# Routing inside the output projection: places taken tile by tile, first two experts' rows built on chip

## The chip, the cores and the metric

One core of a Trainium2 chip runs the kernel. The metric is the device time in microseconds (us), the median of several runs. TensorE (PE), VectorE (DVE), ScalarE (ACT), GpSimd (POOL) and SyncE (SP) run their own instruction streams and meet at semaphores. SP issues the weight DMAs.

## The reference, cut to what matters

Two layers, each a token mixer and a mixture of experts, over 512 tokens of width 1024:

```python
x = x + mix                                   # layer 0: convolution module, layer 1: attention
h = rms_norm(x, norm2_g[i])
x = x + hierarchical_moe(h, ...)              # best group of 4, then top 2 of its 8 experts
# per token and picked expert: gate * (silu(h @ w1[e]) * (h @ w3[e])) @ w2[e]
# 32 experts, each three matrices of 1024 x 512 (2 MB in float32), all float32
```

Both layers read all 96 expert matrices, about 200 MB each.

## The kernel before, in words

Tokens lie in NT = 4 tiles of 128. A weight unit is one 2 MB matrix. There are ten places for units: a ring of six, and four "extra" places that share memory with other data (`area3`, `hT`, `area1`, `area2`). SP issues unit loads in a fixed order; each waits until the work that used its place is done (`to_ring`, `to_extra` in `moe_weights`).

**The join of mixer and experts** (twice, once a layer). `mix_out` is the last projection of the mixer, in two halves of 512 columns, and per half four tiles of eight 512-wide matmuls (L1296). DVE adds each tile to the residual (`add_mix`, L931); ACT makes the norm (L627 to L633) and stores the normed rows `xn` to DRAM; PE transposes them (`transpose_xn`, L1197), DVE scales them into `hT` (`take_hT`, L846), and PE forms the routing logits of the tile (`logits`, L1313, L1314: 8 matmuls of 36 columns and one of the bias). After the logits of all four tiles `route` runs: DVE picks group and experts for all tiles at once (L945 to L976), PE counts ranks with triangular ones (L1322, L1325), DVE turns ranks into slots and lists (L979 to L1008), PE and DVE make the list of rows (L1329, L1011), and POOL gathers the rows of experts 0 and 1 from DRAM (L551). PE runs four matmuls to hold its clock (`stay_warm`, L1204), transposes the gathered rows (L1340), DVE copies them (L1034), and the first expert's matmuls start (`up`, L1350).

**The experts.** Each has 64 slots. A step of PE is `up` of expert e (32 matmuls, L1350), `hid_T` of e-1 (L1358), `rows_T` of e+1 (L1340), `down` of e-1 (L1367). ACT takes silu (L703) and the result (L707), POOL gathers rows (L529) and scatters results to DRAM (L540). Tokens over 64 in an expert go into extra tiles (`over_tile`); in these data layer 0 has one and layer 1 none. At the end ACT loads the results (L739) and DVE adds them (L1082).

Trace names: `banks` is PSUM, `scratch` and `area` are working memory, `ring` the ring of units.

## Time and profile before

| | us |
|---|---|
| median of 3 runs | 1643.52 (1643.09 to 1645.52) |
| the profiled execution | 1641.64 |
| its span, first to last instruction | 1639.5 |
| PE busy | 1389.2 (85% of the span) |
| DVE / ACT / POOL busy | 449.2 / 329.3 / 272.6 |

The two stretches in which all sixteen DMA engines are busy are the two expert stages. In between, and before the first, they stand almost idle. The mean granted PE clock is 0.932 of full.

### The profile page before, as it was taken

What the parts mean: (1) busy time and instruction counts of PE and PEld (TensorE: products, weight loads), DVE (VectorE), ACT (ScalarE), POOL (GpSimd) and SP (SyncE); (2) the same over time, 40 slices, a digit from 0 to 9 for tenths busy, and PEclk for the clock granted to TensorE, in tenths of its full rate; (3) what the DMA queues carried; (4) which work ended last, traced back from release to release, by engine and by line L of the source; (5) the groups of instructions that cost most, each with busy time, mean ns of one, the idle gap of its engine ahead of it and who ended that gap; (6) DMA issues with size and microseconds to landing.
All of it is one profiled execution on the core that took longest, in us unless ns stands there. A gap on an engine that the chain in (4) does not pass through costs nothing.

```text
span 1639.5 us, 16522 instructions
## 1 busy us (share of the span) xinstructions
PE 1389.2 (85%) x6006; PEld 631.7 (39%) x6006; DVE 449.2 (27%) x859; ACT 329.3 (20%) x638; POOL 272.6 (17%) x373
## 2 busy tenths in 40 slices
PE   6998896988888888884799999996998888888883
PEld 3443453333332232231556666544333233223231
DVE  1898424110110110110444544425111011011012
ACT  3564230110000000000444444421100000000000
POOL 3787001121111111110000000001121111111110
PEclk9999896998999999998899999996999999999997
DMA  8322046899999999999500401226899999999994
GB/s 293 93 103 103 0 154 247 362 425 426 426 427 426 426 426 424 424 375 356 204 0 1 154 1 52 103 90 264 351 409 427 426 427 426 426 417 424 415 425 193
DMA packets 62540, 473.63 MB, mean 289 GB/s; under 512 B 15800, under 2 KB 15800, under 8 KB 36512
## 3 DMA queue, kind: packets, MB, share of 16 engines
q1 hardware_dynamic: 49792, 443.63, 65.9%
q0 software_dynamic: 10400, 16.82, 2.7%
q10 hardware_dynamic: 2304, 12.58, 2.0%
q8 instruction: 29, 0.48, 0.1%
q14 instruction: 15, 0.12, 0.0%
HBM read 466.95 MB, written 23.33 MB: 299 GB/s over the span
## 4 chain that ended last, share of the span: by engine, by line
PE 50%; DMA 35%; DVE 7%; POOL 2%; issue 2%; ACT 2%; SPq 1%; ACTq 0%; POOLq 0%; DVEq 0%
DMA ring<-in_moe_w 33%; PE banks L1350 19%; PE banks L1460 6%; PE banks L1296 4%; PE banks L1367 4%; PE banks L1489 3%; POOL scratch L519 2%; DVE banks L892 2%; PE banks L1209 2%; PE banks L1282 2%; PE banks L1549 2%; PE banks L1504 1%; PE banks L1229 1%; DMA area<-y_dram 1%; PE banks L1313 1%
## 5 line engine op out<-in xcount | busy, mean ns | idle before, releaser
L1350 PE MATMUL banks<-ring,scratch 128*64 128x512 f32 x1984 | 493.7, 648 | 137.7 <-DMA ring<-in_moe_w 126.8
L1350 PEld LDWEIGHTS banks<-ring,scratch 128*64 128x64 f32 x1984 | 158.4, 148 | 469.4 <-issue 469.4
L1044 DVE COPY scratch<-banks 128x256 f32<-128x256 f32 x65 | 27.6, 425 | 786.9 <-PE banks L1358 786.9
L1367 PE MATMUL banks<-ring,scratch 128*64 128x512 f32 x1008 | 230.2, 598 | 3.0 <-DVE scratch L1044 3.0
L703 ACT ACTIVATE scratch<-banks 64x512 f32<-64x512 f32 x65 | 38.3, 589 | 585.5 <-PE banks L1350 585.5
L537 POOL COPY at_out<-rows_out 128x1 int32 (+1 forms) x64 | 11.7, 183 | 685.9 <-ACT scratch L707 685.9
L1460 PE MATMUL banks<-hT,ring 128*128 128x512 f32 x256 | 117.9, 604 | 0.8 <-DVE hT L846 0.8
L1209 PE MATMUL banks<-hT,ring 128*128 128x512 f32 x256 | 113.1, 601 | 5.3 <-DMA ring<-in_conv_w_in 5.3
L1367 PEld LDWEIGHTS banks<-ring,scratch 128*64 128x64 f32 x1008 | 68.1, 136 | 117.4 <-issue 110.4
L519 POOL TENSOR_TENSOR scratch<-scratch 128x512 f32<-128x512 f32 x77 | 98.0, 1274 | 23.2 <-ACT scratch L670 12.9
L707 ACT ACTIVATE scratch<-banks 128x512 f32<-128x512 f32 x65 | 38.8, 597 | 284.3 <-PE banks L1367 284.3
L892 DVE SCALAR_TENSOR_TENSOR banks<-scratch,chan,banks 128x512 f32<-128x512 f32 x119 | 79.1, 748 | 0.0
L540 POOL DMA_INDIRECT y_dram<-scratch,at_out x64 | 65.4, 1022 | 56.5 <-POOL at_out L537 56.5
L1209 PEld LDWEIGHTS banks<-hT,ring 128*128 128x128 f32 x256 | 48.8, 193 | 65.9 <-issue 65.8
L529 POOL DMA_INDIRECT scratch<-xn_dram,at_in x60 | 63.2, 1053 | 52.5 <-POOL at_in L526 47.7
L547 POOL MEMSET scratch<- 128x512 f32 x4 | 2.1, 525 | 418.5 <-DVE x_res L931 418.4
L670 ACT ACTIVATE scratch<-scratch,chan 128x512 f32<-128x512 f32 x84 | 58.3, 717 | 36.0 <-POOL scratch L519 25.4
L1460 PEld LDWEIGHTS banks<-hT,ring 128*128 128x128 f32 x256 | 46.2, 189 | 49.3 <-issue 46.9
L1489 PEld LDWEIGHTS banks<-ring,hT 128*128 128x128 f32 x512 | 59.0, 192 | 3.8 <-issue 3.8
L1296 PE MATMUL banks<-ring,area 128*128 128x512 f32 x136 | 59.6, 594 | 0.9 <-DVE area L1180 0.9
L1489 PE MATMUL banks<-ring,hT 128*128 128x128 f32 x512 | 59.6, 275 | 0.0
L1358 PEld LDWEIGHTS banks<-ident,scratch 64*128 64x128 f32 x260 | 35.9, 209 | 54.3 <-issue 54.3
(215 smaller groups left out, 1197.4 us busy)
## 6 DMA issues: line engine op xcount, KB each, us to landing
ring<-in_moe_w SPq DMA_DIRECT2D x187, 2048.0 KB, 20.8
area<-in_moe_w SPq DMA_DIRECT2D x6, 2048.0 KB, 12.2
ring<-in_attn_w_qkv SPq DMA_DIRECT2D x6, 2048.0 KB, 17.0
ring<-in_conv_w_in SPq DMA_DIRECT2D x4, 2048.0 KB, 14.2
area<-y_dram ACTq DMA_DIRECT2D x8, 1024.0 KB, 8.0
ring<-in_conv_w_out SPq DMA_DIRECT2D x2, 2048.0 KB, 21.2
xn_dram<-area ACTq DMA_DIRECT2D x8, 512.0 KB, 2.6
hT<-in_moe_w SPq DMA_DIRECT2D x2, 2048.0 KB, 7.7
```

Source lines behind the costliest of these rows:

```text
L519: g.tensor_tensor(pacc[ct % 2], pacc[ct % 2], tap[(k - 1) % TAP_BUFS], ALU.add).then_inc(tap_added, 1)
L529: g.indirect_dma_start(out=xe[s], out_offset=None, in_=xn_dram[l][:, :], in_offset=bass.IndirectOffsetOnAxis(ap=at_in[:, s:s + 1], axis=0) ...
L540: g.indirect_dma_start(out=y_dram[l][:, :], out_offset=bass.IndirectOffsetOnAxis(ap=at_out[:, s:s + 1], axis=0), in_=y_sb[s], in_offset=No ...
L670: a.activation(dst, u_buf[ct % 2][:, w:w + T], ACT.Copy, scale=chan[:, ct, w:w + 1]).then_inc(tap_made, 1)
L707: a.activation(y_sb[s], bank[6 + s][:], ACT.Copy).then_inc(sems["y_taken"], 1)
L892: ins = v.scalar_tensor_tensor(dst, ub[:, w:w + T], chan[:, ct, w:w + 1], acc, ALU.mult, ALU.add)
L1209: last = mm(dst, w[:, c, cols], src[:, c, :], start=start and c == 0, stop=stop and c == NC - 1)
L1296: last = mm(dst[:], src[:, c, t * P:(t + 1) * P], w_chunks(n0 + n)[:, c, :], start=c == 0, stop=c == NC - 1)
L1350: last = mm(bank[2 + s][q * SLOTS:(q + 1) * SLOTS, :], xeT[s][:, j, h, :], w[:, c, :], start=c == 0, stop=c == NC - 1)
L1367: last = mm(bank[6 + s][q * SLOTS:(q + 1) * SLOTS, :], hidT[s][:, j, :], w2c[:, j, q * 512:(q + 1) * 512], start=j == 0, stop=j == 3)
L1460: last = mm(qk_bank[c][:], w_chunks(u)[:, k, (h % 4) * P:(h % 4 + 1) * P], hT[:, k, :], start=k == 0, stop=k == NC - 1)
L1489: last = mm(v_bank[:, t * P:(t + 1) * P], hT[:, k, t * P:(t + 1) * P], w_chunks(u)[:, k, (h % 4) * P:(h % 4 + 1) * P], start=k == 0, stop= ...
```

## The change

What it does, in the order of the program:

- **Places.** The extra places are taken in another order. `hT` no longer serves the experts' routing, so it takes a unit as soon as the mixer has read it, and `area3` takes one when the mixer is done with it; `area2` at the end of the projection; `area1` after both the stores of `xn` and the building of the first rows.
- **Logits and picks tile by tile.** PE transposes the residual itself (not the normed rows), two matmuls into the next tile's projection, and makes the logits one matmul later. DVE scales the logits by the norm when it reads them and picks for one tile (`choose`, 16 instructions). The bias matmul is gone.
- **Ranks of tiles 0 and 1** are counted inside the last tile's projection, ahead of the logits of tile 2. DVE's `slots` makes their slots there.
- **First rows on chip.** The rows of experts 0 and 1 are no longer gathered from DRAM. `first_rows` builds them, already transposed, by matmuls of `xn` with a 0/1 matrix of 128 columns: 16 matmuls for tiles 0 and 1, 16 for tiles 2 and 3, after two 512-wide fp16 matmuls that clear two banks.
- **Warming matmuls:** four before; now one after the projection and one between the two parts of `first_rows`.
- **End of the experts.** `up` of the last expert is put ahead of `down` of the third last, and the last seven unit loads are reordered to fit. `last_scatter` copies its list column ahead of its wait for the result, not behind it.

PE at the end of the projection and in the routing, layer 0 (128x512 `ring,area` is the projection, `w_route` the logits), before:

```order
L1296 MATMUL banks_3<-ring,area 128x512 x8
L1197 MATMUL banks_7<-ident,area 128x128 x8
L1313 MATMUL banks_5<-w_route,hT 128x36 x8
L1314 MATMUL banks_5<-b_route,ones 128x36
L1197 MATMUL banks_7<-ident,area 128x128 x8
L1313 MATMUL banks_5<-w_route,hT 128x36 x8
L1314 MATMUL banks_5<-b_route,ones 128x36
L1313 MATMUL banks_5<-w_route,hT 128x36 x8
L1314 MATMUL banks_5<-b_route,ones 128x36
L1322 MATMUL banks_5<-scratch,before 128x32
```

and now, from the last tile's projection on:

```order
L1343 MATMUL banks_3<-ring,area 128x512
L1363 MATMUL banks_5<-w_route,scratch 128x36 x8
L1343 MATMUL banks_3<-ring,area 128x512 x5
L1251 MATMUL banks_3<-x_res,ident 128x512
L1245 MATMUL banks_7<-ident,x_res 128x128 x8
L1363 MATMUL banks_5<-w_route,scratch 128x36 x8
L1382 MATMUL banks_1<-ones,zero 128x512 x2
L1389 MATMUL banks_1<-scratch,area 128x128 x16
L1371 MATMUL banks_5<-scratch,ones 128x32 x2
L1371 MATMUL banks_5<-scratch,before 128x32
```

Three logits groups stood behind the projection but for one; now one does, and the row-building matmuls stand between it and the ranks.

PE from the lists to the first experts, before:

```order
L1329 MATMUL banks_5<-scratch 128x47 x8
L1333 MATMUL banks_7<-scratch 128x47 x8
L1204 MATMUL banks_7<-x_res,ident 128x512 x4
L1340 MATMUL banks_1<-ident,scratch 128x128 x8
L1350 MATMUL banks_3<-ring,scratch 64x512 x32
```

and now:

```order
L1375 MATMUL banks_5<-scratch,ones 128x32 x4
L1251 MATMUL banks_3<-x_res,ident 128x512
L1389 MATMUL banks_1<-scratch,area 128x128 x16
L1405 MATMUL banks_5<-scratch 128x47 x8
L1427 MATMUL banks_3<-ring,scratch 64x512 x16
```

Between the row list and the first `up` nothing is left; the transposes of gathered rows are gone and the second list stands behind the first `up`.

The diff, cut to what the prediction speaks of:

```diff
+                to_extra(2, w1_of(3), *((glu_ready, 8), (v_ready, HEADS))[l])
+                to_extra(0, w3_of(2), *((ln_done, NC), (oT_done, HEADS))[l])
                 to_ring(4, w2_of(0), *freed[4])
                 to_ring(5, w1_of(2), *freed[5])
-                to_extra(0, w3_of(2), mix_ready, 8 * (l + 1))
-                to_extra(1, w2_of(1), logits_ready, l + 1)
-                to_extra(2, w1_of(3), xn_stored, 16 * NT * (l + 1))
-                to_extra(3, w3_of(3), xe_loaded[l][1], 16)
+                to_extra(1, w2_of(1), mix_ready, 8 * (l + 1))
+                sp.wait_ge(xn_stored, 16 * NT * (l + 1))
+                to_extra(3, w3_of(3), main[l]["xT_ready"], 2)
...
+                def last_scatter(s, e, wait_at):
+                    pool.wait_ge(y_stored[l][s], 16 * (e // 2))
+                    g.tensor_copy(at_out[:, s:s + 1], rows_out[:, e:e + 1]).then_inc(at_copied[l], 1)
+                    pool.wait_ge(at_copied[l], wait_at)
+                    pool.wait_ge(m["y_taken"], e + 1)
...
                             ins.then_inc(x_done, 1)
+                            take_hT(N_MOE[l], t)
                             invert_rms(N_MOE[l], t)
-                            if t >= 1:
-                                take_hT(N_MOE[l], t - 1)
-                take_hT(N_MOE[l], NT - 1)
+                            if t == NT - 2:
+                                slots(l, 0, NT - 2)
+                            if t < NT - 1:
+                                choose(l, t)
...
+                            if n == 1 and t >= 1 and c == 1:
+                                transpose_xn(N_MOE[l], t - 1)
+                                if t == NT - 1:
+                                    ranks(l, 0, NT - 2)
+                            if n == 1 and t >= 1 and c == 2:
+                                logits(l, t - 1)
                         last.then_inc(mix_ready, 1)
-                        if n == 1 and t >= 1:
-                            transpose_xn(N_MOE[l], t - 1)
-                        if n == 1 and t >= 2:
-                            logits(l, t - 2)
+                stay_warm(1, warm_bank)
                 transpose_xn(N_MOE[l], NT - 1)
-                logits(l, NT - 2)
-                logits(l, NT - 1)
...
+            def first_rows(l, lo, hi):
+                if lo == 0:
+                    for b in range(2):
+                        mm(first_pair[l][:, b, :], zero16[:], ones16[:, 0:1].to_broadcast([P, 512]), ...)
+                pe.wait_ge(xn_done, 4 * N_MOE[l] + hi)
+                pe.wait_ge(hot_first_done, 2 * l + (1 if hi < NT else 2))
+                for j in range(4):
+                    for h in range(2):
+                        k = 2 * j + h
+                        for t in range(lo, hi):
+                            last = mm(first_pair[l][:, k // 4, ...], xn[:, t, ...], hot_first[:, t]..., ...)
             def route(l):
-                pe.wait_ge(picks_done, l + 1)
...
+                logits(l, NT - 1)
+                pe.wait_ge(x_done, 8 * l + NT)
+                pe.wait_ge(picks_done, NT * l + NT - 1)
+                first_rows(l, 0, NT - 2)
+                ranks(l, NT - 2, NT)
+                stay_warm(1, warm_bank)
+                first_rows(l, NT - 2, NT)
                 pe.wait_ge(hot_done, 2 * l + 1)
...
-                stay_warm(4, bank[7])
...
-                rows_step(0, 0)
-                rows_step(1, 1)
                 up_step(0, 0, in_ring(0), in_ring(1))
+                lists2(l)
...
-                step(EXPERTS - 2, 0, in_ring(MOE_UNITS - 7), in_ring(MOE_UNITS - 6), in_ring(MOE_UNITS - 5))
-
-                up_step(EXPERTS - 1, 1, in_ring(MOE_UNITS - 4), in_ring(MOE_UNITS - 3))
+                up_step(EXPERTS - 2, 0, in_ring(MOE_UNITS - 7), in_ring(MOE_UNITS - 6))
+                hid_T(m, 1, EXPERTS - 2)
+                rows_step(EXPERTS - 1, 1)
+                up_step(EXPERTS - 1, 1, in_ring(MOE_UNITS - 5), in_ring(MOE_UNITS - 4))
                 hid_T(m, 0, EXPERTS - 1)
+                down_step(EXPERTS - 3, 1, in_ring(MOE_UNITS - 3))
                 down_step(EXPERTS - 2, 0, in_ring(MOE_UNITS - 2))
```

On DVE the order of the routing is now, for all four tiles: `choose` of 0, 1, then `slots` of tiles 0 and 1, `choose` of 2 and 3, `slots` of 2 and 3, the lists as before, and a copy of each expert's first rows (`take_first`) behind `hot_done` and behind the row list.

## Rows read from the trace of the kernel before

**Rows 1.** Chain in order of time, layer 1 experts: start us, us, what.
```profile
1204.94 19.35 DMA ring<-in_moe_w
1224.52 8.80 PE banks L1350 x32
1233.92 21.70 DMA ring<-in_moe_w
```

**Rows 2.** Stretch sums: us, PE, PEld, DVE, ACT, POOL busy, PEclk, DMA share, GB/s.
```profile
1230.00:1605.00 375.00, 311.08 (x1358) 113.73 (x1356) 43.36 (x72) 28.46 (x48) 56.48 (x92) 0.94 1.00 420
```

**Rows 3.** Timeline, layer 1, projection's end to logits: start, us, engine, line, [idle before].
```profile
1108.12 0.69 DVE L931 TENSOR_TENSOR x_res<-x_res,banks 128x512 f32<-128x512 f32 x1 [6.48 <-PE banks L1296]
1108.87 1.87 PE L1313 MATMUL banks<-w_route,hT 128*128 128x36 f32 x16
...
1113.32 3.47 PE L1313 MATMUL banks<-w_route,hT 128*128 128x36 f32 x16
1113.57 0.69 DVE L846 TENSOR_TENSOR hT<-banks,norm_g 128x512 f32<-128x512 f32 x1 [0.16 <-PE banks L1197]
```

**Rows 4.** The same, layer 1, ranks to the first expert.
```profile
1128.33 0.29 DVE L979 COPY scratch<-banks 128x128 f32<-128x128 f32 x1 [0.58 <-PE banks L1325]
...
1128.88 0.39 DVE L982 TENSOR_TENSOR scratch<-scratch,steps 128x224 f32<-128x224 f32 x1
...
1129.99 0.19 DVE L985 TENSOR_TENSOR scratch<-scratch 128x32 f32<-128x32 f32 x1
1130.21 0.42 DVE L988 TENSOR_TENSOR scratch<-scratch 128x256 f32<-128x256 f32 x1
...
1135.59 0.55 DVE L1006 TENSOR_TENSOR scratch<-scratch,token 128x376 f16<-128x376 f16 x1
...
1143.37 13.95 PE L1350 MATMUL banks<-ring,scratch 128*64 128x512 f32 x64 [0.46 <-DVE scratch L1034]
```

**Rows 5.** Timeline, layer 0, the same two ends.
```profile
238.03 0.69 DVE L931 TENSOR_TENSOR x_res<-x_res,banks 128x512 f32<-128x512 f32 x1 [6.49 <-PE banks L1296]
...
274.92 0.65 PE L1350 MATMUL banks<-ring,scratch 128*64 128x512 f32 x2 [0.46 <-DVE scratch L1034]
```

**Rows 6.** Chain in order of time: 128-wide matmuls; a tile of the projection.
```profile
873.28 3.57 PE banks L1489 x32
...
1091.15 6.87 PE banks L1296 x16
```

**Rows 7.** Timeline, layer 1: transposes of one tile.
```profile
1107.92 1.12 PE L1197 MATMUL banks<-ident,area 128*128 128x128 f32 x8
```

**Rows 8.** Stretch sums, columns as in rows 2, round changes of the clock.
```profile
791.00:794.70 3.70, 3.29 (x14) 2.92 (x15) 2.34 (x6) 3.33 (x5) 0.00 (x0) 0.50 1.04 389
794.80:798.00 3.20, 2.42 (x8) 1.17 (x7) 2.51 (x10) 0.21 (x1) 0.00 (x0) 1.00 1.05 393
```

**Rows 9.** Stretch sums, layer 1, from the projection's end.
```profile
1108.00:1112.00 4.00, 3.33 (x29) 3.17 (x28) 2.04 (x4) 2.59 (x4) 1.05 (x2) 1.00 0.77 229
1112.00:1116.00 4.00, 4.00 (x22) 4.00 (x21) 1.38 (x2) 1.28 (x1) 0.00 (x0) 0.52 0.99 421
```

**Rows 10.** DMA view, issues by line: median us to landing.
```profile
scratch<-xn_dram,at_in POOLq DMA_INDIRECT x61, 9.0
```

**Rows 11.** Chain in order of time, end of layer 1.
```profile
1598.61 7.09 PE banks L1350 x32
...
1606.92 3.65 PE banks L1367 x16
...
1616.32 0.20 POOL at_out L537
...
1617.36 2.34 DMA y_dram<-scratch,at_out
```

**Rows 12.** Chain in order of time, end of layer 0, its extra tile.
```profile
739.80 10.26 DMA ring<-in_moe_w
```

More of the change, by code:

```diff
@@ L742, in _ @@
             route(0)
[L743 removed]
+            act.wait_ge(lists2_done, 1)
             experts(0)
@@ new lines, in slots @@
+            def slots(l, lo, hi):
+                dve.wait_ge(ranks_ready, 2 * l + (1 if hi < NT else 2))
+                n = hi - lo
+                ranks = rank_bank[l][:, lo * EXPERTS:hi * EXPERTS].rearrange("p (t e) -> p t e", e=EXPERTS)
+                first = slice(lo, hi)
+                link(v.tensor_scalar(miss[:, first, :], both[:, first, 0:2], -float(FAR), float(FAR), ALU.mult, ALU.add))
+                link(v.tensor_tensor(place[:, first, :], ranks[:, :, 0:2], miss[:, first, :], ALU.add))
+                v.tensor_tensor(hot_first[:, first].rearrange("p t e s -> p (t e) s"),
+                                iota_slot[:, 0:SLOTS].unsqueeze(1).to_broadcast([P, 2 * n, SLOTS]),
+                                bt(place[:, first, :].rearrange("p t e -> p (t e)"), SLOTS), ALU.is_equal).then_inc(hot_first_done, 1)
+                link(v.tensor_tensor(tmp_kte[:, :, lo:hi, :], picks_kte[:, :, lo:hi, :],
+                                     ranks.unsqueeze(1).to_broadcast([P, 2, n, EXPERTS]), ALU.mult))
+                link(v.tensor_reduce(slot_kt[:, :, lo:hi], tmp_kte[:, :, lo:hi, :], AX.X, ALU.add))
@@ new lines, in take_first @@
+            def take_first(l, s):
+                m = main[l]
+                dve.wait_ge(m["xT_ready"], 2)
+                v.tensor_tensor(xeT[s].rearrange("p j h k -> p (j h) k"), first_xT[l][:, :, s, :], gain_jh[N_MOE[l]],
+                                ALU.mult).then_inc(m["xT_taken"], 1)
+            def route(l):
+                choose(l, NT - 1)
+                slots(l, NT - 2, NT)
+                v.tensor_tensor(g_dif, lg[:, :, 0:GROUPS], bt(v4(0), GROUPS), ALU.subtract).then_inc(exp_in, 1)
@@ L1196, in transpose_xn @@
                     for j in range(4):
[L1197 to L1198 removed]
+                        src = x_res[:, t, 4 * h + j:4 * h + j + 1017:8] if raw else xn[:, t, h * 512 + j:h * 512 + j + 509:4]
+                        last = nc.tensor.transpose(bank[6 + h][:, j * P:(j + 1) * P], src, ident[:])
                     last.then_inc(xt_ready, 1)
@@ L1318, in route @@
-            def route(l):
-                pe.wait_ge(picks_done, l + 1)
-                for t in range(NT):
-                    for u in range(t + 1):
-                        mm(bank[4][:, t * EXPERTS:(t + 1) * EXPERTS], ones16[:] if u < t else before16[:], both[:, u, :],
-                           start=u == 0, stop=u == t)
-                for u in range(NT):
-                    last = mm(bank[4][:, P:P + EXPERTS], ones16[:], both[:, u, :], start=u == 0, stop=u == NT - 1)
-                last.then_inc(ranks_ready, 1)
+                    last = mm(dst, hT_moe[t % 2][:, c, :], w_route[:, l, c, :], start=c == 0, stop=c == NC - 1)
@@ new lines, in logits, with ranks @@
+                last.then_inc(logits_ready, 1)
+            def ranks(l, lo, hi):
+                pe.wait_ge(picks_done, NT * l + hi)
+                for t in range(lo, hi):
+                    for u in range(t + 1):
+                        last = mm(rank_bank[l][:, t * EXPERTS:(t + 1) * EXPERTS], ones16[:] if u < t else before16[:], both[:, u, :],
+                                  start=u == 0, stop=u == t)
+                if hi == NT:
+                    for u in range(NT):
+                        last = mm(rank_bank[l][:, P:P + EXPERTS], ones16[:], both[:, u, :], start=u == 0, stop=u == NT - 1)
+                last.then_inc(ranks_ready, 1)
@@ new lines, in first_rows @@
+            def first_rows(l, lo, hi):
+                if lo == 0:
+                    for b in range(2):
+                        mm(first_pair[l][:, b, :], zero16[:], ones16[:, 0:1].to_broadcast([P, 512]), start=True, stop=False, skip_group_check=True)
+                pe.wait_ge(xn_done, 4 * N_MOE[l] + hi)
[3 more added lines that the diff above has]
+                        k = 2 * j + h
+                        for t in range(lo, hi):
+                            last = mm(first_pair[l][:, k // 4, k % 4 * P:(k % 4 + 1) * P], xn[:, t, h * 512 + j:h * 512 + j + 509:4],
+                                      hot_first[:, t].rearrange("p e s -> p (e s)"), start=False, stop=t == NT - 1,
+                                      skip_group_check=True)
+                if hi == NT:
+                    last.then_inc(main[l]["xT_ready"], 2)
```

168 lines of the change are left out of this document (88 added, 80 removed).

## The prediction

> **What bounds the kernel now.** Read the chain that ended last first, in order of time. In each expert stage it starts as a chain of matmuls and from some expert on alternates between the wait for a weight unit and that expert's 32 matmuls [rows 1]. The landings at the ends of the two DMA pieces there, 1204.94 + 19.35 = 1224.29 and 1233.92 + 21.70 = 1255.62, lie 31.33 us and six units apart: 5.22 us a unit. From there to the end the DMA engines are full (share 1.00, 420 GB/s [rows 2]). So an expert stage ends at a fixed distance behind the point at which the stream got going, and that is set by the first `up`: before 1224 PE runs its first seven experts without waiting for units, and each load waits for a place that these matmuls free. Whatever starts the first `up` earlier moves the whole stream, once in each layer. Faster matmuls later on bring nothing.
>
> Then the timelines between the last projection tile and the first `up`, which is where the change works. Layer 1: DVE adds the last tile at 1108.12 [rows 3] and `up` starts at 1143.37 [rows 4], 35.25 us. Layer 0: 238.03 to 274.92 [rows 5], 36.89 us. Nearly all of it is a single thread through DVE and PE with one thing waiting for the other; DMA is not its limit.
>
> **The change, part by part (layer 1; the clock taken as full first).**
>
> Inside the projection. A tile's eight matmuls take 6.87 us [rows 6]. Before, two groups of transposes (1.12 us each [rows 7]) and one of logits (1.87 [rows 3], with the bias some 2.3) stood among them: 4.5 us. Now three transposes and three logits do, 3 x (1.12 + 1.87) = 9.0, with a wait of about 0.2 each in which DVE scales the second half (0.69 [rows 3]) behind one 0.43-us-per-pass projection matmul, and 0.2 for the early ranks: 9.8. The projection ends **5.3 us later**. DVE's `choose` is 16 dependent instructions of 4 to 36 columns; a 32-column one takes 0.19 and the next starts 0.22 behind it [rows 4], so 3.5 us. It has the last five chunks (5/8 of 6.87 = 4.3 us) as its cover; 0.8 us is left before the next add. If that cover is gone, each excess is paid three times.
>
> Behind the projection, in order:
> - add of the last tile, 0.69 and the handover: 0.75 [rows 3];
> - transposes 1.12 and DVE's second half 0.69, with handovers: 2.1 [rows 7, 3];
> - logits of tile 3: 1.9 [rows 3];
> - `first_rows` of tiles 0 and 1, which PE does before the ranks: 16 matmuls of 128 columns, 3.57 as in the attention's value projection [rows 6]. The two clearing matmuls are fp16 and 512 wide; no row has one. A float32 one of 512 takes two passes of 0.43 [rows 6]; I take 0.3 each, between 0.2 and 0.86: 4.2 together. `choose` of tile 3 (3.5) runs beside it and is hidden, by 0.7;
> - ranks: DVE waited 0.58 us for 14 such matmuls [rows 4]: 0.6 for 11;
> - `slots` and two small instructions: two narrow ones, one of 256 columns (0.42, pitch 0.46), two of 128 (0.29), and 0.4: 1.9 [rows 4];
> - DVE's list chain: 1128.88 to 1136.14 is 7.26 before [rows 4]; two instructions of 256 columns (0.46 each with the gap) move into `slots`: 6.35. Under it PE does one warming matmul and the other 16 matmuls of `first_rows`, about 4.5 us, hidden by 1.9;
> - the copy of expert 0's rows, 0.69 and the handover: 0.8.
>
> Sum 18.6, against 35.25: 16.65 less; minus the 5.3 of the projection, **11.35 us**. Layer 0 has the same work and was 1.64 us longer before: **13.0 us**. Gone are the row gather, the four warming matmuls, the transposes of gathered rows and three quarters of the picks. Together 24.35.
>
> The places taken early I cost at nothing, either way. Their loads use idle DMA time in both kernels, and the first that PE could wait for is an operand of expert 2, two `up`s (13.95 us [rows 4]) behind the start. The price of losing that cover is one unit, 5 us. The third expert's rows are still gathered, see the rivals. The first unit to be issued behind the first `up` keeps its distance to it, so the stream shifts with it.
>
> End of layer 1. The last expert's third matrix now stands one unit earlier in the stream, 5 us; `down` of the third last (3.65) now follows its `up` instead of filling a wait, and the 0.6 us that PE waited there for DVE's copy (1605.70 to 1606.92 less four transposes [rows 11]) is filled: 5.0 - 3.65 + 0.6 = 1.9. `last_scatter` copies its column early: 1616.32 to 1617.36 [rows 11] is 1.0. **2.9 us.** End of layer 0: the extra tile's second matrix is issued when `down` of the second last expert ends, at 739.80 [rows 12], and that comes some 1.6 us earlier against the stream; the rest of that tail is unchanged: **1.6 us.**
>
> **The clock.** Behind the projection the granted clock falls: 1.00 in 1108 to 1112, 0.52 in 1112 to 1116 [rows 9], after 3.3 us busy with transposes and logits only; the same logits group then takes 3.47 instead of 1.87 [rows 3]. In the changed kernel there are two thin stretches: four us round the last transposes and logits, and four us between the end of `first_rows` and the first `up`, in which only eight tiny matmuls run. Between them comes dense work, so I expect each fall to be short. A single `up` that begins on the low level took 8.80 instead of 6.87 to 7.09 [rows 1, 11], 1.7 to 1.9. I charge 1.8 for the first `up` in both layers (nothing covers it), and 1.7 once for the logits stretch, which is about as likely to fall as not: 5.3.
>
> A window of the trace speaks to one rule. In 791.0 to 794.7 PE did nothing but transposes, busy 3.29 of 3.70 us at 0.50, and in the next stretch the clock was 1.00 [rows 8]. The Trainium skill (TensorE: Matmul & The Clock Gate, "Part 4: PE-mode transpose") says that transposes do not count as activity for the full clock. This trace disagrees. By the rule the last transposes would not help to hold the clock and the fall at the logits would come in both layers: 1.7 us more.
>
> **Sum.** 24.35 + 2.9 + 1.6 - 5.3 = 23.5. From the profiled execution's 1641.64: 1618.1. That execution is 1.9 us below the median of the runs (1643.52), against which the result is told: **1620.0**.
>
> **Rivals.**
> 1. *Full clock throughout.* Dense matmuls stand on both sides of each thin stretch. Then 28.8 less: 1614.7. Against it: the fall in four us of the same kind of work.
> 2. *Low clock through the routing.* Logits 1.6 more, clearing and the first 16 matmuls 3.8 more (they are on the path, ahead of the ranks), first `up` 1.8: 7.2 a layer. 28.8 - 14.4 = 14.4 less: 1629.1. For it: before, it stayed low until the warming matmuls. Against it: `first_rows` is as dense as the value projection, which ran at full clock.
> 3. *The gather of the third expert is late.* It cannot start before the row list, which now comes only when `up` starts. Copy, wait and issue take 2.3 us, landing 9.0 [rows 10], and PE wants the rows 14.5 us behind: 3 us to spare. If it lands 5 late, 2 us a layer and as much again on the next: 1625 to 1628.
> 4. *DVE becomes the bound inside the projection.* At 0.30 instead of 0.22 an instruction `choose` is 4.8 us, 0.5 over its cover three times, and 0.6 over `first_rows`: 2.1 a layer, 1624.
> 5. *Slower: the stream's pace.* The two stages hold some 150 units behind the point where DMA takes over. If the loads, reordered at the end and issued against other work, landed every 5.38 instead of 5.22 us, the 0.16 would eat 24 us; at 5.45 the kernel takes 1654. It decides from 0.16 a unit. Against it: the steady loop's loads and gathers are the same, and the engines are full already.
> 6. *The change does not do what it says:* the first `up` waits as long as before, for a unit or for a list. Then only the ends are left, 1639. Nothing in the order of instructions speaks for it.
>
> **How the numbers follow.** Forecast 1620.0 with its neighbours 1617 to 1623: 0.52. Rival 1: 0.14. Rival 2: 0.14. Rivals 3 and 4: 0.11. Rival 5: 0.04, 6: 0.03, and 0.02 for anything else. The range goes from 1612.5 (rival 1 and 2 us for handovers priced too high) to 1629.5 (rival 2); it leaves out about 1 in 10 and holds the clearing matmuls' bounds (1 us). About 0.2% is what a measurement of this kernel can tell from no change. Faster 0.93, same 0.03, slower 0.04.
>
> **What would show it.** From the last add to the first `up` 18 to 22 us in both layers instead of 35 and 37; the last projection tile 5 us later; the first `up` in one piece of 7 to 9 us; the same 5.2 us a unit in the full stretches; PE done some 5 us behind the last landing instead of 7. The prediction is wrong if PE waits between `first_rows` and the lists for DVE longer than 6 us, if a gather stands ahead of the third expert, or if the landings spread.

## The result, and the profile after

| | before | after |
|---|---|---|
| median of 4 runs, us | 1643.3 (1640.1 to 1645.5) | 1624.16 (1623.1 to 1625.1) |
| ratio, 95% interval | | 0.988 (0.987 to 0.990) |
| the profiled execution, us | 1641.64 | 1624.74 |
| its span, us | 1639.5 | 1622.9 |
| last add of the projection to the first `up`, layer 0 and 1, us | 36.89, 35.25 | 22.52, 22.52 |

Faster by 1.2%, inside the range, and 4.2 us above the forecast of 1620.0. From profile to profile it is 16.9 us less where the sum had 23.5, so the sum was 6.6 us too hopeful. That the medians show only 4.2 of it is luck: the profiled execution before lay 1.9 us under the median that the forecast started from, and the one after lies 0.6 us over its own.

The timeline of the changed kernel in layer 1, from the last add to the first `up` (start us, us, engine, line, operation, what it waited for), answers [rows 3, 4]:

```profile
1105.95 0.69 DVE L957 TENSOR_TENSOR x_res<-x_res,banks 128x512 f32<-128x512 f32 x1 [0.47 <-PE banks L1343]
...
1110.66 0.60 PE L1382 MATMUL banks<-ones,zero 128*128 128x512 f16 x2
1111.10 7.52 PE L1389 MATMUL banks<-scratch,area 128*128 128x128 f32 x32
...
1118.92 0.17 DVE L1005 TENSOR_SCALAR scratch<-scratch 128x4 f32<-128x4 f16 x1 [4.20 <-PE banks L1375]
...
1119.89 7.70 PE L1389 MATMUL banks<-scratch,area 128*128 128x128 f32 x32
...
1127.63 0.69 DVE L1017 TENSOR_TENSOR scratch<-banks,gain_sb 128x512 f32<-128x512 f32 x1 [0.84 <-PE banks L1389]
...
1128.47 7.09 PE L1427 MATMUL banks<-ring,scratch 128*64 128x512 f32 x32 [0.68 <-DVE scratch L1017]
```

One kind of row is out of scale: `first_rows` (L1389) takes 7.52 us for 16 matmuls, where 3.57 was forecast. DVE had picked for tile 3 and stood idle for 4.20 us until the ranks (L1375), which PE has queued behind that group. The second group is slow as well, and ends just behind DVE's list chain: DVE waits 0.84 us for it.

Layer 0, the same view; the first two rows are from inside the projection, the end of DVE's `choose` and the next add:

```profile
222.62 0.19 DVE L997 TENSOR_TENSOR scratch<-scratch 128x32 f16<-128x32 f32 x1
223.33 0.69 DVE L957 TENSOR_TENSOR x_res<-x_res,banks 128x512 f32<-128x512 f32 x1 [0.52 <-PE banks L1343]
...
243.21 0.69 DVE L957 TENSOR_TENSOR x_res<-x_res,banks 128x512 f32<-128x512 f32 x1 [0.46 <-PE banks L1343]
...
248.36 7.52 PE L1389 MATMUL banks<-scratch,area 128*128 128x128 f32 x32
...
257.16 7.71 PE L1389 MATMUL banks<-scratch,area 128*128 128x128 f32 x32
...
265.74 8.78 PE L1427 MATMUL banks<-ring,scratch 128*64 128x512 f32 x32 [0.68 <-DVE scratch L1017]
```

Same durations, except for the first `up`: 8.78 against 7.09. Stretch sums of the changed kernel (columns as in [rows 2]):

```profile
248.80:252.10 3.30, 3.30 (x16) 3.30 (x16) 2.72 (x14) 0.12 (x1) 0.00 (x0) 0.50 1.01 417
265.80:269.20 3.40, 3.40 (x10) 1.16 (x12) 2.52 (x7) 0.00 (x0) 1.39 (x2) 0.50 0.97 318
1111.20:1118.40 7.20, 7.20 (x33) 7.20 (x32) 3.03 (x15) 0.46 (x1) 0.00 (x0) 1.00 1.01 425
1128.50:1135.50 7.00, 7.00 (x33) 2.60 (x33) 2.58 (x7) 0.00 (x0) 1.26 (x2) 1.00 0.88 325
1230.00:1590.00 360.00, 299.36 (x1306) 109.46 (x1304) 42.64 (x71) 27.25 (x46) 52.88 (x87) 0.94 1.00 420
```

In layer 0 the first group of rows ran for 3.3 us on the lower level of the clock, in layer 1 on the upper one throughout, and took 7.52 both times. So the clock is not what paces it. PEld, the loads of the stationary operand, is busy without a gap in both. The view by source line (ns, lowest/median/highest) shows these loads in the changed kernel, and in the kernel before for the value projection whose 3.57 us [rows 6] priced the term:

```profile
L1389 PEld LDWEIGHTS banks<-scratch,area x128: 308/329/332, 248.1 to 1127.1; 128*128 128x128 f32 x128
```
```profile
L1489 PEld LDWEIGHTS banks<-ring,hT x512: 190/192/192, 812.0 to 1037.5; 128*128 128x128 f32 x171
```

329 ns a load against 192. `first_rows` takes as stationary operand every fourth column of `xn` (16 bytes apart), the value projection columns side by side. In both a float32 product loads its operand twice (x128 for 64 matmuls).

The step alone is not the whole of it, and the kernel before gave no hint: its transposes read `xn` with the same step of 16 bytes and take 0.14 us each [rows 7]. In the changed kernel the transposes of the residual read columns 32 bytes apart, load once each, and are about as quick:

```profile
1106.70 1.16 PE L1245 MATMUL banks<-ident,x_res 128*128 128x128 f32 x8
```
```profile
L1245 PEld LDWEIGHTS banks<-ident,x_res x64: 185/190/207, 214.5 to 1107.5; 128*128 128x128 f32 x64
```

The end of layer 1, timeline of the changed kernel, answers [rows 11]:

```profile
1568.94 8.78 PE L1427 MATMUL banks<-ring,scratch 128*64 128x512 f32 x32 [3.27 <-issue]
...
1579.06 0.69 DVE L1079 TENSOR_TENSOR scratch<-banks,gain_sb 128x512 f32<-128x512 f32 x1 [0.25 <-PE banks L1417]
...
1579.90 7.09 PE L1427 MATMUL banks<-ring,scratch 128*64 128x512 f32 x32 [0.87 <-DVE scratch L1079]
...
1595.85 3.65 PE L1444 MATMUL banks<-ring,scratch 128*64 128x512 f32 x16 [0.61 <-DVE scratch L1089]
...
1599.60 0.60 ACT L729 ACTIVATE scratch<-banks 128x512 f32<-128x512 f32 x1 [4.28 <-PE banks L1444]
...
1601.04 0.98 POOL L554 DMA_INDIRECT y_dram<-scratch,at_out  x1 [3.69 <-ACT scratch L729]
```

and the chain at the end of layer 0, answering [rows 12]:

```profile
731.42 10.99 DMA ring<-in_moe_w
```

### The profile page after: what moved, and what is told of

Read it like the earlier page. It is cut to its first block, busy times and chain, and to the rows that moved or that the text cites. A ratio compares the mean times of both kernels' runs of the same rounds, so it can differ in the third digit from the quotient of the medians.

```text
span 1622.9 us, 16775 instructions
## 1 busy us (share of the span) xinstructions
PE 1401.9 (86%) x6098; PEld 643.0 (40%) x6098; DVE 466.7 (29%) x957; ACT 329.0 (20%) x638; POOL 268.1 (17%) x370
## 4 chain that ended last, share of the span: by engine, by line
PE 51%; DMA 36%; DVE 6%; POOL 2%; issue 2%; ACT 2%; SPq 1%; ACTq 0%; POOLq 0%; DVEq 0%
DMA ring<-in_moe_w 33%; PE banks L1427 19%; PE banks L1539 6%; PE banks L1444 4%; PE banks L1568 4%; PE banks L1343 3%; POOL scratch L533 2%; PE banks L1389 2%; DVE banks L918 2%; PE banks L1256 2%; PE banks L1329 2%; PE banks L1628 2%; PE banks L1583 1%; PE banks L1276 1%; DMA area<-y_dram 1%
## 5 line engine op out<-in xcount | busy, mean ns | idle before, releaser
L1427 PE MATMUL banks<-ring,scratch 128*64 128x512 f32 x1984 | 496.2, 650 | 137.9 <-DMA ring<-in_moe_w 128.1
L566 POOL DMA_INDIRECT y_dram<-scratch,at_out x58 | 59.6, 1028 | 51.3 <-POOL at_out L563 51.3
## 6 DMA issues: line engine op xcount, KB each, us to landing
ring<-in_attn_w_qkv SPq DMA_DIRECT2D x6, 2048.0 KB, 18.6
hT<-in_moe_w SPq DMA_DIRECT2D x2, 2048.0 KB, 14.9
```

The source lines that it names most:

```text
L566: g.indirect_dma_start(out=y_dram[l][:, :], out_offset=bass.IndirectOffsetOnAxis(ap=at_out[:, s:s + 1], axis=0), in_=y_sb[s], in_offset=No ...
L1427: last = mm(bank[2 + s][q * SLOTS:(q + 1) * SLOTS, :], xeT[s][:, j, h, :], w[:, c, :], start=c == 0, stop=c == NC - 1)
```

## The experiments

The theory: the step in the read of `first_rows`' stationary operand costs about 4 us a layer, since the ranks stand behind the first group. The rivals: the accumulation into eight places, or the one-hot operand, is slow; or something else of the route is. The step of the transposes speaks for these. Beyond that, each other part of the change was undone by itself.

All runs in one table, from their timelines. "Route" is last add to first `up` in layer 0 / 1; "stage 0" the first `up` to the first transposes of layer 1; "attention" from there to the last add of layer 1; "stage 1" the first `up` to the end. Medians are of four runs each, and each ratio is to runs of the kernel before on the same chip. The runs come from several chips, on which the kernel before took 1642.0 us (the changed kernel again, and columns side by side, 8 and 32 bytes apart), 1644.3 (expert norm only, early `up`, rows gathered, ranks late) and 1642.5 (new end, places late, old end, no warming). So a median of one group is compared with one of another by the ratios, and their intervals are some 0.0015 to 0.003 wide to each side, 2.5 to 5 us.

| kernel | median us | ratio to before | route | stage 0 | attention | stage 1 |
|---|---|---|---|---|---|---|
| before | 1643.3 | 1 | 36.9 / 35.3 | 508.8 | 324.4 | 496.1 |
| after | 1624.2 | 0.988 | 22.5 / 22.5 | 510.6 | 329.6 | 494.4 |
| after, again | 1624.0 | 0.989 | 22.5 / 22.5 | 508.5 | 329.4 | 494.7 |
| columns side by side | 1623.6 | 0.989 | 19.4 / 19.4 | 511.0 | 333.1 | 495.5 |
| columns 8 bytes apart | 1621.8 | 0.988 | 19.5 / 18.0 | 510.4 | 332.8 | 497.0 |
| columns 32 bytes apart | 1626.4 | 0.991 | 22.8 / 22.8 | 511.2 | 329.7 | 494.9 |
| 8 bytes, expert norm only | 1620.9 | 0.985 | 18.0 / 19.5 | 511.6 | 331.4 | 496.5 |
| the same and early `up` | 1613.7 | 0.981 | 17.2 / 15.7 | 509.2 | 329.6 | 496.5 |
| the same and new end | 1613.2 | 0.982 | 15.7 / 17.2 | 510.8 | 331.1 | 493.4 |
| rows gathered | 1628.5 | 0.990 | 25.4 / 25.4 | 508.5 | 329.6 | 494.8 |
| ranks late | 1627.2 | 0.989 | 23.5 / 23.5 | 508.5 | 331.9 | 494.2 |
| places late | 1626.0 | 0.990 | 22.5 / 22.5 | 511.2 | 329.6 | 495.0 |
| old end | 1627.7 | 0.991 | 22.5 / 22.5 | 511.1 | 329.6 | 496.2 |
| no warming matmuls | 1623.4 | 0.988 | 22.5 / 22.5 | 508.4 | 332.1 | 495.0 |

**The changed kernel again.**

> The changed kernel again, unaltered, as the measure for the other runs on this chip. Both theories: about 1624 us (1624.16 us in its first runs, 0.988 of the kernel before), the 16 matmuls of first_rows 7.5 and 7.7 us in each layer, and the first up matrix 22.5 us behind the projection's last add.

1624.0 us, ratio 0.989 (0.988 to 0.991): as before. But stage 0 is 2.1 us shorter than in the first profile of the very same program; differences of that size in a stage are looked at below.

**Columns side by side.**

```diff
-    a.activation(xn[:, t, :].rearrange("p (h q j) -> p h q j", ...), x_res[:, t, :].rearrange("p (q h j) -> p h q j", ...
+    a.activation(xn[:, t, :].rearrange("p (h j q) -> p h j q", ...), x_res[:, t, :].rearrange("p (q h j) -> p h j q", ...
-    last = mm(first_pair[l]..., xn[:, t, h * 512 + j:h * 512 + j + 509:4],
+    last = mm(first_pair[l]..., xn[:, t, h * 512 + j * P:h * 512 + (j + 1) * P],
```

> The normalised rows are stored so that the 128 columns which one matmul of first_rows takes as stationary operand lie side by side, where they now lie 4 floats (16 bytes) apart; nothing else changes. Theory A, the step in the read of the stationary operand sets the pace of first_rows: its weight loads fall from 329 to about 192 ns each, as attention's value projection has them with operands side by side, and its groups of 16 matmuls from 7.52 and 7.70 us to about 3.6 us each. The ranks, which wait behind the first group and were 3.9 us late, and the first up matrix come some 3.9 to 4.8 us earlier in each layer, the kernel about 8 to 9 us sooner: 1615 us. The Trainium skill (page SBUF - State Buffer, section Specifications (TRN2)) has cache lines of 16 bytes and wants two hits in each; with it theory A holds, since 4 floats are one line. Theory B, it is the accumulation into eight places of two banks in turn, or the small one-hot moving operand: first_rows stays at 7.5 us and the kernel at 1624 us. Against both: the normalisation on ScalarE, now reading with a step of 8 floats and writing side by side, may take longer than its 1.148 us.

Weight loads by line, and the route of layer 1 in the timeline:

```profile
L1389 PEld LDWEIGHTS banks<-scratch,area x128: 186/192/337, 247.7 to 1121.6; 128*128 128x128 f32 x128
```
```profile
1111.53 5.36 PE L1389 MATMUL banks<-scratch,area 128*128 128x128 f32 x32
...
1118.16 3.81 PE L1389 MATMUL banks<-scratch,area 128*128 128x128 f32 x32
...
1125.81 8.62 PE L1427 MATMUL banks<-ring,scratch 128*64 128x512 f32 x32 [0.32 <-DVE scratch L1017]
```

The load is 192 ns and the second group 3.81 us: theory A holds for the matmuls, B is out. The first group took 5.36 us, since the clock stood at its lower level for some 3 us of it (0.53 from 1111.7 to 1115.0): once the read no longer paces it, the clock does. The route is 3.1 us shorter in each layer. Yet the kernel gained nothing: 1623.6 us where theory A had 1615. The normalisation, by line, and the transposes and first projection of layer 1's attention in the timeline, show where it went:

```profile
L655 ACT ACTIVATE area<-x_res,small x16: 2133/2147/2175, 6.9 to 1109.3; 128x1024 f32<-128x1024 f32 x16
```
```profile
784.65 1.97 PE L1245 MATMUL banks<-ident,area 128*128 128x128 f32 x8 [1.77 <-ACT area L655]
787.40 12.35 PE L1539 MATMUL banks<-hT,ring 128*128 128x512 f32 x24 [0.78 <-DVE hT L872]
```

ScalarE's normalisation takes 2.15 us instead of 1.15: the step has been moved into its read. Ahead of attention PE waits for it at every tile; from the first transposes to the first projection it is 14.1 us (773.27 to 787.40) against 12.4 in the changed kernel, and that projection takes 12.35 instead of 10.57. Against the second profile of the changed kernel the two routes won 6.2 us; attention lost 3.7, stage 0 2.5 and stage 1 0.8, the last two with first `up`s of 8.6 us on the lower level instead of 7.1.

**Columns 8 bytes apart**, the normalisation in two instructions (columns `j // 2 * 256 + j % 2`, step 2).

> As the run with the columns side by side, but 2 floats (8 bytes) apart, and the normalisation of a tile in two instructions. If what costs is that each element lies in a line of 16 bytes of its own, half of the elements now share one: first_rows at 3.6 us as with columns side by side, and the kernel near 1615 us. If any step costs in proportion, first_rows lies between, at 5 to 6 us, and the kernel near 1619 us. If the step is not the cause, 7.5 us and 1624 us.

```profile
L1391 PEld LDWEIGHTS banks<-scratch,area x128: 192/196/336, 247.4 to 1119.1; 128*128 128x128 f32 x128
```
```profile
1110.32 3.92 PE L1391 MATMUL banks<-scratch,area 128*128 128x128 f32 x32
...
1115.51 4.01 PE L1391 MATMUL banks<-scratch,area 128*128 128x128 f32 x32
...
1122.47 0.50 PE L1407 MATMUL banks<-scratch 128*128 128x47 f16 x8 [2.95 <-DVE scratch L1051]
1123.16 9.81 PE L1429 MATMUL banks<-ring,scratch 128*64 128x512 f32 x32 [0.19 <-DVE scratch L1019]
```
```profile
L656 ACT ACTIVATE area<-x_res,small x32: 741/754/773, 6.9 to 1108.7; 128x512 f32<-128x512 f32 x32
```

196 ns: with 8 bytes the read is as quick as side by side. The normalisation of a tile is 1.42 us in the timeline, its two instructions overlapping a little. At full clock (layer 1) the route is 18.0 us, 4.5 less than in the changed kernel, and PE now waits 2.95 us for DVE's list chain. The first `up` then fell on the lower clock level and took 9.81 us.

**Columns 32 bytes apart.** `first_rows` reads the residual, so this kernel leaves out the norm's scale for experts 0 and 1.

```diff
-    last = mm(first_pair[l]..., xn[:, t, h * 512 + j:h * 512 + j + 509:4],
+    last = mm(first_pair[l]..., x_res[:, t, 4 * h + j:4 * h + j + 1017:8],
```

> first_rows reads the residual in place of the normalised rows, so experts 0 and 1 get rows without the norm's scale; the step is then 8 floats (32 bytes) instead of 4, and all else is the same. The transposes of the residual, which also step by 8 floats, took 0.13 us each in the trace, at full clock. If one element for each line of 16 bytes is what costs, step 8 is as slow as step 4: 7.5 us and 1624 us. If it costs by the width of the step, more than 7.5 us and later than 1624 us. If a step of 16 bytes alone is bad (elements that fall on the same part of the memory), first_rows drops to 3.6 us and the kernel to 1615 us.

```profile
L1389 PEld LDWEIGHTS banks<-scratch,x_res x128: 312/336/337, 248.6 to 1128.9; 128*128 128x128 f32 x128
```

336 ns, as with 16 bytes, and 7.7 and 7.9 us a group. So in `first_rows` 4 bytes give 192, 8 bytes 196, 16 bytes 329, 32 bytes 336: the cost jumps between 8 and 16 and is flat on either side. The Trainium skill (SBUF — State Buffer, "Specifications (TRN2)") says that SBUF has 16-byte lines and that a reader needs two hits in each for full bandwidth. The four numbers agree with it. With that rule the changed kernel's groups would have been priced above the value projection's.

The transposes do not follow these four numbers. Those of the gathered rows (16 bytes apart in the changed kernel, side by side in the run of that name) load in 211 and 141 ns:

```profile
L1417 PEld LDWEIGHTS banks<-ident,scratch x244: 196/211/220, 282.4 to 1578.6; 128*128 128x128 f32 x122
```
```profile
L1417 PEld LDWEIGHTS banks<-ident,scratch x244: 137/141/144, 278.7 to 1575.8; 128*128 128x128 f32 x122
```

With 8 bytes it is 209, and four of them take 0.66, 0.74 and 0.75 us at 4, 8 and 16 bytes. So any step costs a transpose a little, and none doubles it. Why a product pays so much more for the same step stays open.

**8 bytes apart for the expert norms alone**; the norm ahead of attention as in the changed kernel.

> The expert norms alone write their rows 2 floats (8 bytes) apart, in two instructions of 0.7 us; the norm ahead of attention keeps the order of the changed kernel, where it takes 1.15 us and not 1.43. Theory A (what the run with 8 bytes everywhere won at the routes, it lost ahead of attention: from the layers' join to the logits of layer 1 it took 337.3 us and not 334.2, because the norm holds up TensorE and its clock rises later): the routes stay as in that run (4.0 us a group, the first up matrix some 15.0 us behind the logits in place of 17.9), the stretch from the join to the logits falls back to 334.2 us, and the kernel comes at 1621.8 - 3 = 1618.8 us. Rival: the stretch stays at 337 us and the kernel at 1621.8 us; then the loss comes from another place than the norm.

1620.9 us with runs from 1615.8 to 1624.6, too wide to tell from the forecast of 1618.8 or the rival's 1621.8. The trace is clearer, though it is of the slowest of the four. Of the 3.1 us that attention had lost with 8 bytes everywhere, 1.4 came back, so theory A holds for less than half. The stretch from the first transposes to the first projection is at 12.4 us (775.43 to 787.82), where 8 bytes everywhere had 12.65: the norm itself had cost 0.3 there. The rest is the clock. The first projection in the timeline and its start in the stretch sums, of this kernel and then of the changed one:

```profile
787.82 12.30 PE L1546 MATMUL banks<-hT,ring 128*128 128x512 f32 x24 [0.78 <-DVE hT L879]
...
787.90:791.30 3.40, 3.40 (x4) 1.43 (x5) 1.36 (x7) 0.21 (x1) 0.00 (x0) 0.50 1.05 389
```
```profile
788.71 10.57 PE L1539 MATMUL banks<-hT,ring 128*128 128x512 f32 x24 [0.79 <-DVE hT L872]
...
788.80:792.20 3.40, 3.40 (x8) 1.54 (x9) 1.35 (x7) 0.20 (x1) 0.00 (x0) 1.00 1.05 388
```

The same work behind the same transposes starts at the lower level here and at the upper one there: 1.7 us.

**Early `up`:** 8 bytes for the expert norms, and the first expert ahead of the lists.

```diff
+                take_first(l, 0)
                 link(v.tensor_tensor(hot_slot, iota_slot[:]...
...
-                take_first(l, 0)
```

and the eight matmuls of the row list now stand between the second and third chunk of the first `up`.

> As the run with the expert norms 8 bytes apart, and the first up matrices are started ahead of the row lists: expert 0's rows are taken into SBUF before the wide comparisons of VectorE, and the matmuls of the lists go between the up matmuls. In the run with 8 bytes TensorE stood idle for 2.95 us in this place, with the first group of rows long there. Theory A (with first_rows quick, VectorE's chain to the lists is what the first up waits for): up starts 2.9 us earlier in each layer and the expert stream with it, 5.5 to 6 us sooner in all, at 1613 us. Rival B: the lists come later by the 0.7 us of the copy and by the matmuls ahead of them, the gather of expert 2 with them, and TensorE waits at expert 2 instead; gain 0 to 2 us. Rival C: the start wins, and the weight stream, which sets the pace behind it, gives it back at the places not yet free: gain under 2 us.

```profile
1110.49 4.01 PE L1396 MATMUL banks<-scratch,area 128*128 128x128 f32 x32
...
1115.84 2.80 PE L1436 MATMUL banks<-ring,scratch 128*64 128x512 f32 x12 [1.35 <-DVE scratch L1024]
1118.57 0.37 PE L1414 MATMUL banks<-scratch 128*128 128x47 f16 x8
```

1613.7 us, ratio 0.981 (0.979 to 0.983), expected 1613. The route is 15.7 us in layer 1 and 17.2 in layer 0, where the first group of rows met 3.4 us of low clock. Only 1.35 us of PE's wait is left. The number came by another way than theory A's: the two routes are 4.6 us shorter than in the run before, not 5.8, and stage 0 and attention gave 2.4 and 1.8 more, since the first `up`s (7.5 us for 9.70 and 8.51) and the first projection (10.57 for 12.30) kept the upper level. Stage 1 is 2.1 us longer than in the changed kernel. Its last `up` starts 451.4 us behind the first as there, but took 8.69 us instead of 7.09, and that is 1.6 of it. This beats both kernels, by 10 us the changed one.

**The same and a new end:** the last expert's row transposes ahead of the `up` of the one before.

> The run with expert rows 8 bytes apart and the first up matrices ahead of the lists, with the end of the experts changed too: the transposes of the last expert's rows go ahead of the up matrices of the expert before it, so that the last up matrices wait for nothing but their weights. Expected if the 0.70 us in which the last up matrices wait for VectorE's copy of the rows, at the end of layer 1, lie on the path: 0.7 to 0.8 us sooner at the end of layer 1 (29.7 us from the last landing to the end, against 30.5), as much at the end of layer 0, and 1612.2 us against 1613.7. Rival: the last landing of weights sets both ends, and the move is worth nothing: 1613.7 us. On the other side: the up matrices of the expert before it come 0.7 us later, release their ring places later, and the last two transfers with them: 0.7 us slower in a layer, 1614.5 us or more.

1613.2 us, ratio 0.982 (0.981 to 0.984): no difference from the run before that these runs can tell. In the profile stage 1 is 3.1 us shorter, 1.6 of it because the last `up` kept the upper clock level (7.09 us for 8.69), and 1.5 because it starts earlier against the first one (449.9 us for 451.4). Against that, stage 0 is 1.6 us longer. What the move itself is worth stays open.

**Rows gathered** from DRAM for experts 0 and 1 as before; the rest of the change stays.

> The rest of the changed kernel, but the rows of experts 0 and 1 come from DRAM by two gathers as before the change, and are transposed on TensorE; no first_rows. If the on-chip rows bring what is left of them beside their cost (16 reads of 16-byte step in each group, 3.9 us of them on the path ahead of the last ranks, against gathers of some 9 us that start behind the lists), the first up comes about 1.8 us later in each layer and the kernel at 1627 to 1628 us. If the matmuls' cost had eaten all of their gain: 1624 us or below. If the cost on the path is small after all: over 1632 us.

```profile
1123.94 0.50 PE L1405 MATMUL banks<-scratch 128*128 128x47 f16 x8 [7.98 <-DVE scratch L1053]
...
1132.01 7.09 PE L1428 MATMUL banks<-ring,scratch 128*64 128x512 f32 x32 [0.40 <-DVE scratch L1083]
```

1628.5 us. The route is 25.4 us: on-chip rows bring 2.9 us a layer with the slow read (expected 1.8) and 7.4 without it (18.0).

**Ranks late:** those of tiles 0 and 1 and their slots behind the last logits.

> The ranks and slots of tiles 0 and 1 are taken behind the last logits again, as before the change; the rest of the change stands. Theory A (they were some 2 us of TensorE's and VectorE's chain, and lie under the projection when early): first up about 2 us later in each layer, 1627 to 1628 us. Rival: the strided matmuls of first_rows hold the chain in any case, VectorE has 4.2 us idle in that place, and slots of tiles 0 and 1 fit into it: no difference above 0.5 us a layer, 1624 to 1625 us.

1627.2 us, the number of theory A, but its ratio is that of the changed kernel on its own chip (0.989). The route is 1.0 us longer a layer, half of what was expected: PE waits 0.57 us for the slots ahead of the first group. A further 2.3 us stand in the attention stretch (331.9), where the first projection took 12.82 us on the lower clock.

**Old end:** PE, ACT, the weight queue and the overflow waits in the order of before.

> The end of the experts in the order of before the change, on TensorE, ScalarE and in the weight queue; last_scatter stays, and all else of the changed kernel. Forecast's own view: the new order was put at 1.9 us for layer 1 and 1.6 us for layer 0, so 1627.6 us. From the two traces: from the last landing to the end of layer 1 the changed kernel took 29.3 us where before it took 30.9, 0.36 us of it by last_scatter, and layer 0 showed no gain: then 1.2 us slower, 1625.3 us. Rival: 0, 1624 us, with the wait for rows that the new order brings (0.70 us on VectorE's copy) gone as well.

Stage 1 is 496.2 us against 494.4 and 494.7: the new order is worth 1.5 to 1.8 us in layer 1. Total 1627.7, 3.6 us more; the other 2 us are stage 0's (511.1). There the last `up` took 8.78 us on the lower clock level, for 7.09 in the changed kernel's second profile (508.5). Without these 1.7 us some 0.9 is left that may be the order's.

**Places late:** the extra places taken at the mix, the logits and the stored rows, as before.

> The two extra weight places are taken at the same events as before the change (the mix, the logits, the stored rows) and not within the output projection; all else as in the changed kernel. Theory A (expert 0 and 1 had their weights before the change too, and the stream behind them starts at the end of the first up matrices): no difference over 0.5 us, 1624 us, the first up 17.9 us behind the logits, and the last landing 465.1 us behind the first up of layer 1. Rival B: three more matrices have to come while the experts run, each of some 5 us of transfer; with a stream that sets the pace, the last landing comes up to 5 us later in each layer, 1629 to 1634 us.

Route, attention and stage 1 are unchanged; rival B (1629 to 1634) is out. The median is 1626.0 (1622.8 to 1626.8), 2 us over theory A, and by the ratios (0.990 and 0.989) no difference. The profiled run has 2.7 us more, all in stage 0, and there in the last `up` of the 32 experts; this kernel, with its stretch, and the changed kernel's second profile:

```profile
714.60 9.97 PE L1427 MATMUL banks<-ring,scratch 128*64 128x512 f32 x32 [2.35 <-DMA ring<-in_moe_w]
...
714.70:719.60 4.90, 4.90 (x12) 1.50 (x14) 0.00 (x0) 0.00 (x0) 0.00 (x0) 0.50 0.99 421
```
```profile
715.19 7.09 PE L1427 MATMUL banks<-ring,scratch 128*64 128x512 f32 x32 [0.88 <-DMA ring<-in_moe_w]
```

They start 448.7 and 448.8 us behind the first `up`, so the stream had kept its pace; one meets the lower clock level and is 2.9 us longer, with nothing to cover it, as the extra tile's units wait for its places. Places taken early are worth nothing that shows here.

**No warming matmuls:** both `stay_warm(1, ...)` of the route left out.

> The two matmuls of 128x512 that only keep TensorE at work (1.1 us behind the ranks, ahead of the second group of rows, and one in the last logits' place) are left out of the changed kernel. Theory A (they are worth their time): without them the granted clock falls to its lower level in the first up matrices of both layers and these take 8.6 us, as in the runs with quick rows, in place of 7.1: first up 0.8 us earlier and its end 0.7 us later, 1624 to 1626 us. Rival B (the slow reads of first_rows keep TensorE at work by themselves): the second group ends 1.1 us earlier, the first up starts 0.7 to 0.8 us earlier at full clock, since VectorE's last comparison is done 0.84 us ahead of the group's end: 1622.5 us.

```profile
1119.36 7.71 PE L1388 MATMUL banks<-scratch,area 128*128 128x128 f32 x32 [1.01 <-DVE scratch L1007]
```

Both missed. The matmul had filled a wait: the second group cannot start before DVE's one-hot matrix, and waits 1.01 us for it now. The route is the same to 0.01 us, and both first `up`s ran at the upper level. But the clock did fall inside that group, where the changed kernel's first profile has 1.00 throughout:

```profile
1122.00:1125.00 3.00, 3.00 (x14) 3.00 (x14) 2.69 (x10) 0.00 (x0) 0.00 (x0) 0.50 0.02 5
```

The group takes 7.71 us with it and 7.70 without. So the warming matmuls cost nothing; what they may hold of the clock is hidden by the slow reads, and with quick reads it was not tried. Attention is 2.5 us longer (its first projection took 13.03 us), far from any matmul that was left out.

## Why the prediction was right, and where it was off

- **What bounds the kernel: right.** Stage 1 was 496.1 before and 494.4 after, though the first `up` came 14.9 us earlier. The stream moved as one piece, at 420 GB/s and a DMA share of 1.00 as in [rows 2].
- **Inside the projection: right.** The last add of layer 0 is 5.2 us later (238.03 to 243.21), attention to the last add of layer 1 also 5.2. `choose` ended 0.5 us ahead of the next add, not 0.8; rival 4 did not come.
- **The route: the step that failed is "`first_rows` ... 16 matmuls of 128 columns, 3.57 as in the attention's value projection".** It took 7.52. The shape was the same and the row at full clock; how the stationary operand lies in memory was not compared. The statement that the second group was "hidden by 1.9" fell with it: at 7.70 it ended last, by 0.84. The route came at 22.5 us, not 18.6: 3.9 a layer, 7.8 in all. That is 3.95 from the first group and 0.84 from the second, less 0.9 by which the remaining terms were priced too high, most of it in DVE's chain and the wait for the ranks. With the columns 8 bytes apart it is 18.0 at full clock. The clearing matmuls took 0.60 for both, as priced.
- **The clock: charged 5.3, cost 1.7** in the profile of after (the first `up` of layer 0, 8.78 for 7.09). Layer 1 kept the upper level from its first projection to beyond the first experts. Over all profiles the first `up` met the lower level in 6 of 6 places where the reads were quick and PE had idled some 3 us ahead of it for the lists, in 1 of 14 with the slow reads, and in none of 4 with the early `up`. This fits slow reads that also filled PE's wait, so that part of what they cost came back; it is argued from these counts and not shown. The logits that the prediction had its eye on kept the upper level in both layers (1.95 us); the fall in layer 0 came in the first group of rows, where it cost nothing. In the forecast's total 3.6 us won here hide half of the 7.8 lost: luck, as far as the number goes.
- **End of layer 1: 1.6 us for 2.9.** From the last landing to the end it is 29.3 us against 30.9. The run with the old order puts 1.5 to 1.8 on the order as a whole, near the 1.9 of the sum, yet 0.8 to 1.0 of this is an earlier last landing (465.1 and 464.9 us behind the first `up`, for 465.9), and from the landing on it is 29.3 and 29.8 us for 30.3. A wait not in the sum came up: the last `up` is held 0.87 us by DVE's copy of its rows (L1079). `last_scatter` saved 0.36, not 1.0: from the start of ACT's last result to the issue it is 1.44 (1599.60 to 1601.04) for 1.80 before, and 0.60 of this is ACT, 0.84 the issue on POOL, which the early copy does not shorten.
- **End of layer 0: 0 to 0.3 us for 1.6,** and perhaps 0.9 by the run with the old order. In the second profile of the changed kernel, whose first `up` is at full clock as it was before, stage 0 is 508.5 for 508.8. The extra tile's second matrix was issued 1.3 us earlier against the first `up` (463.5 for 464.9), but took 10.7 us (10.99 in the first profile) instead of 10.26 [rows 12], and the third landed 480.2 us behind it as before (480.1). With three loads in a row the landings did not follow the issue.
- **Places at nothing, third gather: right.** No wait for a gather stands ahead of expert 2. The early loads did fill the DMA engines during the route (share 1.01 from 1111.2 to 1118.4 in layer 1), and 0.01 was left from 1119 to 1128.
- **What is left.** 7.8 + 1.3 + 1.6 lost, 3.6 won: 7.1, where the profile was 6.6 short. Of the 0.5 over, 0.2 is the projections (5.2 later, twice, for 5.3), and 0.3 the time outside the span.

## What to carry to other kernels

Price a matmul by a row of the same kind with the same shape and the same step in memory, for the stationary operand as for any other; here every fourth float doubled a group of products, and left the transposes nearly alone. When the step is moved elsewhere, price the instruction that now has it: ScalarE paid a full microsecond a tile where the route had won 3.1 a layer. And when a shorter route stands in front of a stream, look at what the clock does to the first uncovered block of matmuls, since 1.4 to 2.9 us come and go there.

## What the runs showed of the hardware

- The load of a 128x128 float32 stationary operand in a product: 192, 196, 329, 336 ns at steps of 4, 8, 16, 32 bytes. In a transpose: 141, 209, 211, 190 at the same steps. ScalarE, 128x1024 float32: 1.15 us with runs of four floats read, 1.42 with runs of two (two instructions), 2.15 with single floats 32 bytes apart.
- A group bound by such reads takes 7.52 us with 3.3 us of it at the lower clock level or with none; with columns side by side it took 3.81 at the upper and 5.36 with some 3 us at the lower.
- Three uncovered places take the clock's price: the first `up` (7.09 or 8.5 to 9.8), the last `up` of layer 0 (7.09 or 8.8 to 10.0), and the first projection of attention (10.57, or 12.1 to 13.4). Which falls where changes between kernels that do the same work there, and between two profiles of the same kernel. They explain most of the 2 us by which stage 0 and attention differ between profiles. What decides it stays open.
